# The order of a one-core hybrid layer's mixer stages: from a planner's rules to a written table

## The reference, cut to what matters

```python
p = rms_norm(x, norm_mix) @ w_in
# rw: RWKV-7. Token shift of r, k, v, then per head, over t:
m = p + (p_prev - p) * mu
S = S * w_t + (S @ a_t) b_t^T + v_t k_t^T;  y_t = S @ r_t        # LayerNorm, + bonus, * silu(gate)
# cv: u = val * sigmoid(glu); causal depthwise conv of width 31;  # LayerNorm, swish, * silu(gate)
# h:  HGRN2, f = lb + (1-lb) sigmoid(f_pre), chunks of 64;        # RMS, * silu(gate)
# s:  stick-breaking attention, blocks of 128 queries:
A = exp(log_sigmoid(z) + tail_sum(log_sigmoid(-z)));  o = A @ v   # * silu(gate)
x = x + concat(y_rw, y_cv, y_h, y_s) @ w_out
x = x + softmax((rms(x) @ wq) (rms(mem) @ wk)^T / 16) (rms(mem) @ wv) @ wo
out = rms_norm(x, norm_final)
```

## Time and profile before

| | |
|---|---|
| median of 3 runs | 1131.08 us (1128.71 to 1133.42) |
| profiled execution, first to last instruction (span) | 1128.3 us |
| around the span (median less span) | 2.8 us |
| TensorE busy / weight loads busy | 1058.6 us (94%) / 915.3 us (81%) |
| VectorE / ScalarE / GpSimd busy | 576.8 / 415.1 / 288.5 us |
| mean granted TensorE clock | 0.977 |

### The profile page before, as it was taken

The page is one execution under the profiler, slowest core; times in us unless marked ns, Lnnn a source line. Parts: engine busy times, 40 slices in busy tenths (PEclk is TensorE's granted clock), DMA queues, the critical chain, the costliest instruction groups (busy, mean ns, idle before and its releaser), DMA issues.

```text
span 1128.3 us, 25035 instructions
## 1 busy us (share of the span) xinstructions
PE 1058.6 (94%) x10748; PEld 915.3 (81%) x10748; DVE 576.8 (51%) x837; ACT 415.1 (37%) x719; POOL 288.5 (26%) x259
## 2 busy tenths in 40 slices
PE   6999978999899899989989799999989999999997
PEld 5788866886688698768868678888579999999997
DVE  6316998864447734153584875333231175445115
ACT  7314102023644411365534635555530062223033
POOL 3334640011326100113402000451142433422220
PEclk9999989999999999989989899999999999999999
DMA  7111110000111100021100017665551101111104
GB/s 236 36 31 47 47 47 3 3 22 20 30 28 47 29 4 3 2 75 39 39 20 20 2 42 216 200 186 163 193 180 38 48 31 46 58 47 39 38 20 150
DMA packets 83999, 71.16 MB, mean 63 GB/s; under 512 B 4081, under 2 KB 72881, under 8 KB 83890
## 3 DMA queue, kind: packets, MB, share of 16 engines
...
...
## 4 chain that ended last, share of the span: by engine, by line
PE 69%; DVE 18%; ACT 7%; DMA 2%; issue 2%; POOL 1%; SPq 0%; DVEq 0%; ACTq 0%; POOLq 0%
PE units L1103 10%; PE bank L1372 7%; PE bank L1371 7%; PE bank L1373 7%; PE bank L1052 7%; PE bank L1054 6%; PE bank L1053 6%; DVE yT L1676 5%; PE bank L1092 5%; DVE A L1673 3%; ACT A L1392 2%; ACT B L1392 2%; PE duo L1319 2%; DVE late L1676 1%; PE duo L990 1%
## 5 line engine op out<-in xcount | busy, mean ns | idle before, releaser
L1371 PE MATMUL bank<-vhi,act_hi 128*128 128x256 f32 x704 | 200.4, 285 | 0.0
L1372 PE MATMUL bank<-vlo,act_hi 128*128 128x256 f32 x704 | 199.4, 283 | 0.0
L1373 PE MATMUL bank<-vhi,act_lo 128*128 128x256 f32 x704 | 198.1, 281 | 0.0
L1052 PE MATMUL bank<-act_hi,whi 128*128 128x512 f32 x464 | 192.7, 415 | 0.0
L1054 PE MATMUL bank<-act_hi,wlo 128*128 128x512 f32 x464 | 182.8, 394 | 0.0
L1053 PE MATMUL bank<-act_lo,whi 128*128 128x512 f32 x464 | 182.8, 394 | 0.0
L1103 PEld LDWEIGHTS units<-A 64*64 64x64 f32 x4608 | 147.1, 139 | 36.4 <-issue 18.3
L1103 PE MATMUL units<-A 64*64 64x64 f32 x4608 | 155.4, 224 | 22.3 <-DVE A L1839 9.7
L975 POOL TENSOR_SCALAR whi<-wraw 128x512 fp32r<-128x512 f32 x62 | 57.1, 922 | 456.5 <-PE bank L1054 388.4
L1372 PEld LDWEIGHTS bank<-vlo,act_hi 128*128 128x128 f32 x704 | 134.8, 192 | 0.0
L1373 PEld LDWEIGHTS bank<-vhi,act_lo 128*128 128x128 f32 x704 | 134.8, 191 | 0.0
...
## 6 DMA issues: line engine op xcount, KB each, us to landing
...
```

What stands on the lines that cost most here:

```text
L1052: mm(bank, wh, act_hi[:, k, cols], start=k == 0, stop=False)
L1371: mm(bank, ah, vhi[:, (m + 1) % 2, k, :], start=k == 0, stop=False)
L1372: mm(bank, ah, wide_lo(m)[:, k, :], start=False, stop=False)
L1373: ins = mm(bank, al, vhi[:, (m + 1) % 2, k, :], start=False, stop=k == KT - 1)
```

## The change

The planner (costs, ranks, holds) goes. `mixer_chains` keeps the chains with what each link needs, now without costs, and names them by a letter: a and b the RWKV halves, g and h the HGRN2 halves, c the convolution, s and t the stick-breaking halves, m the memory norm. `TILE_ORDER` lists the tiles, and `MERGE` whose turn it is: "p18 a p2" is 18 pieces, one link of chain a, 2 pieces.

```diff
-IDLE = 24.099
-URGENT = (9.221, 25.55, 18.82, 3.275, 0.761, 0.103, 0.069, 1.093)
-TILE_RANK = {t: n for n, t in enumerate((
...
+TILE_ORDER = (
+    ('rw', 0, 'k'), ('rw', 0, 'gate'), ('rw', 0, 'r'), ('cv', 0, 'glu'), ('cv', 0, 'val'), ('s', 0, 'v'),
...
+MERGE = (
+    'p18 a p2 a p64 a2 p4 a p10 c p4 c2 p c p4 c p15 c2 p6 c4 p6 c4 p2 c p6 c2 p8 c2 p3 c2 p6 c4 p4 c2 p2 c p a2 '
...
+    for turn in MERGE.split():
+        for _ in range(int(turn[1:] or 1)):
+            if turn[0] != "p":
+                put(*chains[turn[0]].pop(0))
                 continue
...
+            kind, h, k = pieces.pop(0)
+            put(("piece" if h < 2 else "part",) + kind + (h, k))
+            if k == max(piece_list(kind))[1]:
+                put(("proj",) + kind + (min(h, 1),))
```

More of the change, by code:

```diff
@@ L125, in mixer_chains, with step, halves @@
 def mixer_chains():
-    rec, stick, conv = [], [], []
+    rec, conv, stick = [], [], []
     def proj(*kind):
         return ("proj",) + kind + (1,)
[L134 to L139, removed]
+    def step(chain, stage, *needs):
+        chain.append((stage, ([chain[-1][0]] if chain else []) + list(needs)))
+    def halves(chain, stage, needs):
@@ L140, in halves @@
         for h in range(2):
-            chain.append((stage + (h,), parts, before if waits(h) is None else waits(h)))
-    step(rec, ("xwt",), [("AS", 1.1)], proj("xw"))
+            chain.append((stage + (h,), needs(h)))
+    step(rec, ("xwt",), proj("xw"))
     for i in range(2):
[L145 to L153, removed]
+        step(rec, ("lora", i))
+        step(rec, ("rwa", i), proj("rw", i, "k"), proj("rw", i, "r"))
+        step(rec, ("kkn", i))
+        step(rec, ("rwb", i))
+        halves(rec, ("tok", "v", i), lambda h: [proj("rw", i, "v")])
+        step(rec, ("bon", i))
+        halves(rec, ("tok", "b", i), lambda h: [("rwb", i)])
+        halves(rec, ("tok", "k", i), lambda h: [("rwb", i)])
+        halves(rec, ("minit", i), lambda h: [("rwb", i)])
@@ L169, in mixer_chains @@
+        halves(rec, ("gt", i), lambda h: [("hh", i, h)])
+        halves(rec, ("qq", i), lambda h: [("gt", i, h)])
         for c in range(1, NC - 1):
[L170 removed]
+            step(rec, ("cs", i, c))
             if c in (NC // 2 - 2, NC - 2):
[L172 to L174 removed]
+                step(rec, ("yy", i, c // (NC // 2)), ("cs", i, c))
@@ L175, in mixer_chains @@
+        step(rec, ("var", i))
+        step(rec, ("rfin", i), proj("rw", i, "gate"))
     for i in range(2):
[L176 to L179, removed]
+        step(rec, ("hgate", i), proj("h", i, "f"), proj("h", i, "i"), proj("h", i, "q"))
@@ L180, in mixer_chains @@
+        halves(rec, ("tok", "hv", i), lambda h: [proj("h", i, "i")])
+        halves(rec, ("hdiag", i), lambda h: [("hgate", i)])
         for l in range(6):
[L181 to L191, removed]
+            halves(rec, ("hlev", i, l), lambda h: [("hlev", i, l - 1, h) if l else ("hgate", i)])
@@ L193, in mixer_chains @@
+        step(rec, ("hbars", i), ("hlev", i, 5, 0))
+        halves(rec, ("tok", "hk", i), lambda h: [("hbars", i)] + [("mn", 1)] * (i == 0))
+        halves(rec, ("hkv", i), lambda h: [("tok", "hk", i, h)])
+        halves(rec, ("hout", i), lambda h: [("hkv", i, h)])
+        step(rec, ("hvar", i))
+        step(rec, ("hfin", i), proj("h", i, "gate"))
     for i in range(2):
         for tap in range(CW):
-            step(conv, ("conv", i, tap), [("D", 1.35)], *[proj("cv", i, w) for w in ("glu", "val")])
@@ L196, in mixer_chains @@
[L196 to L199, removed]
+            step(conv, ("conv", i, tap), *[proj("cv", i, w) for w in ("glu", "val")])
+    step(conv, ("cmean",))
+    step(conv, ("csq",))
+    step(conv, ("cvar",))
+    step(conv, ("cfin",), proj("cv", 0, "gate"), proj("cv", 1, "gate"))
@@ L211, in mixer_chains @@
                 if u:
-                    step(stick, ("sbv", i, th, u - 1), [("P", 0.9 * share(u - 1))])
+                    stick.append((("sbv", i, th, u - 1), [("sbt", i, th, u - 1)]))
                 if u < n:
[L214 to L225, removed]
@@ new lines, in mixer_chains, with cut @@
+                    stick.append((("sbt", i, th, u), [("sbz", i, th, u)]))
+            step(stick, ("sbo", i, th), proj("s", i, "gate"))
+    for i in range(2):
+        step(stick, ("ysplit", i), ("rfin", 1), ("hfin", 1), ("cfin",))
+    mem = [(("mn", 0), [("rfin", 1)]), (("mn", 1), []), (("mT", 0), [("mn", 0)]), (("mT", 1), [("mn", 1)])]
+    def cut(chain, *firsts):
+        at = [0] + [n for n, (stage, _) in enumerate(chain) if stage in firsts] + [len(chain)]
+        return [chain[a:b] for a, b in zip(at, at[1:])]
@@ new lines, in mixer_chains, with put @@
+    first, second, h0, h1 = cut(rec, ("lora", 1), ("hgate", 0), ("hgate", 1))
+    s0, s1 = cut(stick, ("sv", 1))
+    return {"a": first, "b": second, "g": h0, "h": h1, "c": conv, "s": s0, "t": s1, "m": mem}
+def mixer_order():
+    chains = mixer_chains()
+    pieces = [(t, 3, k) for t in (("xw",), FIRST_TILE) for k in range(KT)]
+    pieces += [(t, h, k) for t in TILE_ORDER for h, k in piece_list(t)]
+    order, placed = [], set()
+    def put(stage, needs=()):
+        assert all(n in placed for n in needs), (stage, needs)
+        order.append(stage)
+        placed.add(stage)
+    for turn in MERGE.split():
+        for _ in range(int(turn[1:] or 1)):
+            if turn[0] != "p":
+                put(*chains[turn[0]].pop(0))
+                continue
+            kind, h, k = pieces.pop(0)
+            put(("piece" if h < 2 else "part",) + kind + (h, k))
+            if k == max(piece_list(kind))[1]:
+                put(("proj",) + kind + (min(h, 1),))
+    assert not pieces and not any(chains.values())
```

181 lines of the change are left out of this document (11 added, 170 removed), and 20 rows, old and new, of tables (MERGE, TILE_ORDER, TILE_RANK).

## The result

The changed kernel took 1122.15 us (median of 4 runs, 1121.54 to 1123.08) against 1131.7 us for the one before: a ratio of 0.9923, interval 0.9904 to 0.9942, that is -8.7 us (-6.6 to -10.9). Forecast was 1119, -11.9 us, in a range of 1107 to 1130. Run twice more on other chips it came to 0.9873 (0.9847 to 0.9898) and 0.9905 (0.9878 to 0.9931), that is -14.4 and -10.7 us.

A forecast was written before the change was run, and what follows sets the result against it. TensorE was busy 1058.6 of 1128.3 us with its work unchanged, so only its 69.7 us idle and low-clock loss could move. Terms summed to -11.9 us, from 1131.1 to 1119, range 1107 to 1130.

The forecast's parts named there:

- the unit: Unit 0 1 3 moved ahead of yy: its two waits and half the low-clock cost behind go, -6.4 us.
- the end: End of the mixer part: w_out loads start earlier against the output projection, whose waits go, -3.3 us.
- the start: Ahead of lora 0: two more pieces fill part of its 1.90 us wait, -1.4 us.
- the convolution stretch: Solve inputs ready earlier and one tap fewer ahead, so the wait before tok v 0 0 shrinks, -2.5 us.
- `hlev` of the second half: Four pieces come from behind to before its 4.29 us wait for VectorE, -2.4 us.
- `cs`: Steps between which six gaps lose their piece, each then paid elsewhere, +3.7 us.
- `hgate`: At hgate 0 a third table change, a 1.28 us load with nothing before it to hide it, +1.3 us.
- `hvar`: hvar 0 follows hout bare, without the two pieces that stood between, +1.5 us.
- stick-breaking: Stick-breaking and memory tiles: other piece counts, about as many waits shorter as longer, -0.7 us.
- the waits only move: Rival, chance 0.15: pieces brought in front are missed behind, four stretches bring nothing, 1127 us.
- More goes than I count: Rival, chance 0.20: low clock of the stretches from 53.4 and 162.6 goes as well, 1111.5 us.
- Slower by the low clock behind bare places: Rival, chance 0.12: new bare places drop the granted clock, 3.4 us each, 17 in all, 1136 us.

The follow-up runs named there:

- e3_tile: Changed kernel with tile qa 5 taken from between the vo tiles and put ahead of them: 1122.32 us, 0.9923 of the kernel before.
- e9_bunit: Kernel before, its order and tiles, with only unit 0 1 3 moved ahead of yy and var: 1131.65 us, 1.000 of the kernel before.
- c1_after: Changed kernel run again with no edit, in the third series: 1121.25 us, 0.9905 of the kernel before.
- e2_cs: Changed kernel with one piece in each of the six bare gaps between cs steps: 1121.36 us, 0.9879 of the kernel before.
- e4_sbv: Changed kernel with two vo pieces between the last sbt and its sbv: 1118.26 us, 0.9861 of the kernel before.
- e8_hlev: Changed kernel with the pieces around the second half's hlev placed nearly as before: 1120.42 us, 0.9897 of the kernel before.
- e1_unit: Changed kernel with only unit 0 1 3 put back behind yy and var: 1126.83 us, 0.9936 of the kernel before.

## Why the prediction was right, and what was mis-sized

The frame was right: TensorE's work is unchanged, and the time came from its waits and the low clock. The two largest steps held in size, the unit (-6.9 against -6.4) and the end (-3.7 against -3.3), and so did the start and the convolution stretch. That the sum came close is in part luck. The four stretches that should win with the unit and the end (start, convolution, entry, `hlev` of the second half) won 8.3, as forecast (8.0), but all the other rows together took back 9.6 where I had 5.8 (`cs`, `hgate`, `hvar`, less stick-breaking), and 6.4 of that, in the first half's `var` and `hlev` and in `hout` 1, was not forecast at all.

Reasons with a flaw stand behind right sizes too. At the end I gave the gain to the tile at SP's gate, and e3_tile shows that the tile is not what decides. The unit's price holds only beside other edits there (e9_bunit). In `hlev` of the second half the wait fell to 2.62, not to the 1.6 that I named; all waits of the levels together fell from 9.3 to 6.8, and the rest of the -3.4 is in the main low clock. Before `hvar` 0 I had 1.4 of waiting; it is 0.53 before the second `hout` and 0.52 before `hvar`. And of the idle time before, 10.5 us stand in the first 50 and 12.5 behind the mixer part, not about 18 and 5; the sum, and so what an order can win, is the same.

From -11.9 to the -9.3 of the profiles these terms matter most:

*The standstill in `hout` 1.* Not forecast, +1.7 to +4.5 with the low stretch that followed in one of the three profiles. It takes back most of what `hlev` won.

```profile
666.25 3.79 PE L955 MATMUL units<-A 64*64 64x64 f32 x110
672.54 0.74 PE L955 MATMUL units<-A 64*64 64x64 f32 x18 [2.49 <-issue]
```

No engine releases TensorE there ("issue").

*`hgate` 0 and the first `hlev`.* I had +1.3 for a table load with nothing to hide it. The load is there, at 546.18:

```profile
546.18 1.28 ACT L1242 ACT_TABLE_LOAD   x1 [0.88 <-DVE A L1532]
547.48 1.24 ACT L1244 ACTIVATE A<-A,der 128x1024 f32<-128x1024 f32 x1
```

But the new order also lays 12 pieces between `hgate` 0 and `hlev` 0 0 0 instead of 9, two of them directly ahead of it, and the wait there fell from 2.02 to 0.44 (559.60 above). Here it is in e9_bunit, whose order in this place is that of before:

```profile
566.17 1.15 PE L960 MATMUL units<-A 64*64 64x64 f32 x32 [2.02 <-DVE A L1530]
```

Behind it, three pieces fewer between the levels cost 1.8 us. I had counted the load and not the pieces. No run separates the two.

*The `cs` gaps.* +2.7, not +3.7. A bare step is shorter than I took it: I had named six intervals of 1.16. VectorE's steps in c1_after, behind two bare gaps and then a covered one (start, us, line, tiles, idle before):

```profile
461.14 0.28 DVE L1750 SCALAR_TENSOR_TENSOR A<-units,DC,A 128x64 f32<-128x64 f32 x1 [1.99 <-PE units L1086]
462.11 0.28 DVE L1750 SCALAR_TENSOR_TENSOR A<-units,DC,A 128x64 f32<-128x64 f32 x1 [0.69 <-PE units L1086]
462.90 0.28 DVE L1750 SCALAR_TENSOR_TENSOR A<-units,DC,A 128x64 f32<-128x64 f32 x1 [0.50 <-PE units L1086]
464.05 0.28 DVE L1750 SCALAR_TENSOR_TENSOR A<-units,DC,A 128x64 f32<-128x64 f32 x1 [0.87 <-PE units L1086]
```

The bare intervals are 0.97 and 0.79 us, against 1.15 with a piece between, as in the earlier trace rows: in the covered gap it is the piece, 0.90 when alone, that sets the interval, not VectorE alone. A bare gap and its piece elsewhere cost 0.79 + 0.68 = 1.47 or 0.97 + 0.68 = 1.65 against 1.15, +0.3 to +0.5 each, where I had +0.68 less a little.

*`var` 0 to `sbv` 0 1 0.* +1.6, where I had 0. The waits are the same (4.8 and 4.9 us in all); it is low clock. TensorE was busy at half speed for 5.3 us of this stretch before and for 9.2, 6.7 and 8.9 us after, which costs 1.9, 0.7 and 1.8 more. Whether the order brings that, one profile of before can't tell.

*Stick-breaking.* +0.9, where I had -0.7. The last `sbt` has 8 `vo` pieces ahead of it instead of 10, and waits 1.14 (1.59 and 1.57 in the other two profiles) where it did not wait before; against it two waits of 0.8 are gone. My count of "about as many shorter as longer" was no working at all.

*Convolution stretch.* The wait before `tok v` 0 0 fell by 2.65, and part of it returned in the solve behind, as forecast: waits of 1.28 before `mk3` and 0.88 before `qq` are new.

Of the rivals, "the waits only move" is what e2_cs, e4_sbv, e8_hlev and e9_bunit show of single edits. Of the mixer part as a whole it is nearly true: outside the unit what was won at the places named was lost at others. It is false of the unit in the new order (e1_unit) and of the output projection. "More goes than I count": the low stretches from 53 and 162 were halved in some executions, not removed. "Slower by the low clock behind bare places": the mean clock rose, from 0.977 to 0.984, and no low stretch stands in the `cs` steps of the changed kernel's three profiles. But e3_tile, whose `cs` steps are the same, has one that begins behind step 11 of the second half (start and end, sum, busy PE, PEld, DVE, ACT and POOL, granted clock):

```profile
461.90:468.80 6.90, 6.44 (x38) 4.39 (x38) 1.14 (x4) 0.59 (x1) 3.79 (x4) 0.51 0.00 0
```

That costs 3.2 us, the one behind the bare last `sbt` and `sbv` 1.7 where it comes. Such a price may belong to bare places, then, in some executions; it was too small and too rare to decide, and no run shows the cause.

The table load is again 1.28 with the next ACTIVATE 0.02 behind it (546.18 to 547.48): the drain that the Trainium skill's "ScalarE: Activation LUTs", What ACT_TABLE_LOAD costs, adds does not show here either.
